# Projections as one float32 matmul per product, from a ring of 12 landed weight units

## The reference

```python
h = rms_norm(x, norm_mix)
proj = h @ w_in                      # 2048 x (512 + 256 + 64 + 3 * 1024)
# MLA heads: q and k, v from the two latents by w_q_b (512 x 1536) and w_kv_b (256 x 2048)
# stick-breaking heads: q, k, v straight from proj
x = x + concat(rms_norm(o_mla), rms_norm(o_sb)) @ w_out          # 2048 x 2048
x = x + softmax(q_mem k_mem) v_mem @ w_mem_o   # w_mem_q 2048x512, w_mem_kv 2048x1024, w_mem_o 512x2048
x = x + hierarchical_moe(rms_norm(x))          # 32 experts of 512, gate, up and down
y = rms_norm(x)
```

## Time and profile before

| | |
|---|---|
| time, median of 3 runs | 1455.09 us (1454.99 to 1457.09) |
| span of the profiled execution, first to last instruction | 1450.0 us |
| the profiled execution's own time | only its span is given |
| TensorE busy | 1082.5 us, 75% |
| VectorE busy | 540.3 us, 37% |
| ScalarE busy | 337.4 us, 23% |
| mean granted clock of TensorE | 0.893 of full |
| HBM read | 479.04 MB, 332 GB/s over the span |

### The profile page before, as it was taken

How to read it: one execution, slowest core, us unless ns; L and a number is a source line. 1 busy time by engine, 2 the same in 40 slices (tenths; PEclk the granted TensorE clock), 3 DMA queues, 4 the chain that set the end, 5 groups by cost and what they waited for, 6 DMA issues and landing times.

```text
span 1450.0 us, 21354 instructions
## 1 busy us (share of the span) xinstructions
PE 1082.5 (75%) x8717; PEld 643.9 (44%) x8717; DVE 540.3 (37%) x1120; ACT 337.4 (23%) x609; POOL 33.2 (2%) x90
## 2 busy tenths in 40 slices
PE   6999988998998968667656666667656665666665
PEld 5888867777887733222222222223222222222222
DVE  5444556565564433322222222222222222222323
ACT  5554455565444230100000000000000000000002
POOL 1000000110001000000000000000000000000000
PEclk9999999999999988988888888788888898788977
DMA  6766743222655789999999999999999999999996
GB/s 212 268 190 189 185 134 116 87 88 93 209 182 176 322 350 423 428 425 426 428 427 427 423 428 427 427 424 427 427 427 425 426 428 427 427 424 427 427 427 259
DMA packets 85379, 481.69 MB, mean 332 GB/s; under 512 B 10262, under 2 KB 20636, under 8 KB 51932
## 3 DMA queue, kind: packets, MB, share of 16 engines
q1 hardware_dynamic: 84272, 478.70, 82.5%
q10 hardware_dynamic: 876, 2.15, 0.4%
q0 software_dynamic: 192, 0.31, 0.2%
HBM read 479.04 MB, written 2.10 MB: 332 GB/s over the span
## 4 chain that ended last, share of the span: by engine, by line
DMA 47%; PE 41%; ACT 3%; DVE 3%; SPq 3%; issue 1%; POOL 0%; DVEq 0%; ACTq 0%; POOLq 0%
DMA gu<-in_w_up 29%; DMA down<-in_w_down 17%; PE ps L408 8%; PE ps L410 8%; PE ps L409 8%; PE ps L684 5%; PE ps L731 5%; SPq L323 2%; PE ps L665 2%; PE ps L388 1%; PE ps L674 1%; DVE w_lo L1066 1%; PE ps L483 1%; ACT x_slots L1015 1%; DMA x_res<-in_x 1%
## 5 line engine op out<-in xcount | busy, mean ns | idle before, releaser
L684 PE MATMUL ps<-gu,xe 128*32 128x256 f32 x4096 | 317.9, 479 | 232.8 <-DMA gu<-in_w_up 231.8
L684 PEld LDWEIGHTS ps<-gu,xe 128*32 128x32 f32 x4096 | 153.9, 137 | 417.7 <-DMA gu<-in_w_up 279.0
L1461 DVE TENSOR_TENSOR x_res<-ps,x_res 128x512 f32<-128x512 f32 x248 | 153.9, 683 | 406.9 <-PE ps L694 406.9
L408 PE MATMUL ps<-w_hi,a_hi 128*128 128x512 f32 (+1 forms) x552 | 220.5, 399 | 8.6 <-DVE w_lo L1066 3.6
L409 PE MATMUL ps<-w_lo,a_hi 128*128 128x512 f32 (+1 forms) x552 | 215.9, 391 | 0.0
L1066 DVE TENSOR_TENSOR w_lo<-w_raw,w_hi 128x1024 fp32r<-128x1024 f32 (+1 forms) x138 | 163.9, 1200 | 132.0 <-ACT w_hi L772 131.1
L410 PE MATMUL ps<-w_hi,a_lo 128*128 128x512 f32 (+1 forms) x520 | 202.7, 390 | 0.0
L772 ACT ACTIVATE w_hi<-w_raw 128x1024 fp32r<-128x1024 f32 (+1 forms) x138 | 141.8, 1038 | 150.6 <-PE ps L410 142.8
L1022 ACT ACTIVATE sg<-ps 128x128 f32<-128x128 f32 x32 | 8.9, 278 | 625.8 <-PE ps L684 625.8
L731 PE MATMUL ps<-down,turned 128*32 128x512 f32 x1024 | 122.8, 611 | 31.6 <-ACT turned L1028 24.4
L408 PEld LDWEIGHTS ps<-w_hi,a_hi 128*128 128x128 f32 x552 | 106.0, 192 | 29.8 <-ACT w_hi L772 2.5
(11 more groups left out here) (233 smaller groups left out, 685.7 us busy)
## 6 DMA issues: line engine op xcount, KB each, us to landing
gu<-in_w_gate SPq DMA_DIRECT2D x64, 2048.0 KB, 31.7
gu<-in_w_up SPq DMA_DIRECT2D x64, 2048.0 KB, 36.1
down<-in_w_down SPq DMA_DIRECT2D x64, 2048.0 KB, 24.6
w_raw<-in_w_in SPq DMA_DIRECT2D x56, 512.0 KB, 4.0
w_raw<-in_w_out SPq DMA_DIRECT2D x32, 512.0 KB, 4.2
w_raw<-in_w_mem_kv SPq DMA_DIRECT2D x16, 512.0 KB, 3.7
w_raw<-in_w_mem_q SPq DMA_DIRECT2D x8, 512.0 KB, 3.4
w_raw<-in_w_mem_o SPq DMA_DIRECT2D x8, 512.0 KB, 4.4
```

Source lines behind the costliest of these rows:

```text
L408: pe.matmul(acc[t][:, 0:n], xh, wh, start=(k == 0), stop=False)
L684: mm = pe.matmul(ps[5][j * SLOTS:(j + 1) * SLOTS, 0:2 * P].rearrange("s (m f) -> s m f", m=2), xe[:, k, :], gu[side][:, b, :, kk, j * P:(j ...
L1461: ins = ve.tensor_tensor(xs, ps[g][:, :], xs, ALU.add)
```

## The change

The products become one matmul of type float32, on weights as they landed and on activations in one copy. The rounding on ScalarE and the subtraction on VectorE go. The room of `w_raw`, `w_hi` and `w_lo` becomes one ring of 12 units, and SP refills a place when TensorE has used its unit. The turned activations are copied once: banks with an even number by ScalarE, with an odd one by VectorE. `a_hi` and `a_lo` become `a_even` and `a_odd`, two places for whole activations: mix, mem, memx and memo use the first, q, kv and out the second. The order of TensorE's work and all that lies behind the projections are the same.

```diff
-RING = 4
+RING = 12
...
-        a_hi = place("a_hi", [P, KD, SEQ], F32R)
+        a_even = place("a_even", [P, KD, SEQ])
         a_lo_at = at[0]
-        a_lo = place("a_lo", [P, KD, SEQ], F32R)
+        a_odd = place("a_odd", [P, KD, SEQ])
         w_at = at[0]
-        w_raw = place("w_raw", [P, RING, UK, UN])
-        w_hi = place("w_hi", [P, RING, UK, UN], F32R)
-        w_lo = place("w_lo", [P, RING, UK, UN], F32R)
+        w_ring = place("w_ring", [P, RING, UK, UN])
...
+        def copied(b):
+
+            return (S("odd_copied"), b // 2 + 1) if b % 2 else (S("even_copied"), b // 2 + 1)
...
                 if u >= RING:
-                    sp.wait_ge(S("w_split"), u - RING + 1)
-                dst = w_raw[:, u % RING, :, 0:chunk_cols(c)]
+                    sp.wait_ge(S("w_used"), u - RING + 1)
+                dst = w_ring[:, u % RING, :, 0:chunk_cols(c)]
...
                     if b >= 4:
-                        pe.wait_ge(S("split_lo"), 2 * (b - 4) + 2)
+                        pe.wait_ge(*copied(b - 4))
...
-                    pe.wait_ge(S("w_rounded"), u + 1)
-                    pe.wait_ge(S("w_split"), u + 1)
+                    pe.wait_ge(S(f"w_loaded{u % RING}"), landed(u))
                     for j in range(UK):
                         k = i * UK + j
                         for t in range(TT):
-                            xh = hi[:, a0 + k, t * P:(t + 1) * P]
-                            xl = lo[:, a0 + k, t * P:(t + 1) * P]
-                            wh, wl = w_hi[:, u % RING, j, 0:n], w_lo[:, u % RING, j, 0:n]
-                            pe.matmul(acc[t][:, 0:n], xh, wh, start=(k == 0), stop=False)
-                            pe.matmul(acc[t][:, 0:n], xh, wl, start=False, stop=False)
-                            mm = pe.matmul(acc[t][:, 0:n], xl, wh, start=False, stop=(k == kn - 1))
+                            mm = pe.matmul(acc[t][:, 0:n], a[:, a0 + k, t * P:(t + 1) * P],
+                                           w_ring[:, u % RING, j, 0:n], start=(k == 0),
+                                           stop=(k == kn - 1))
                     mm.then_inc(S("w_used"), 1)
...
-            def rounded(upto):
...
-                    sc.activation(w_hi[:, u % RING, :, 0:n], w_raw[:, u % RING, :, 0:n],
-                                  ACT.Copy).then_inc(S("w_rounded"), 1)
...
-            def split_head(name, g0, used=0, a0=0, hi=a_hi, k_from=0, k_to=None):
+            def copy_split(name, g0, used=0, a0=0, a=a_even, k_from=0, k_to=None):
...
+                for kk in range(k_from // 2, (kn if k_to is None else k_to) // 2):
+                    b = k0 // 2 + kk
+                    if b % 2 == 0:
+                        sc.wait_ge(S("split_turned"), b + 1)
+                        for i in range(2):
+                            k = 2 * kk + i
+                            ins = sc.activation(a[:, a0 + k, :], ps[4 + b % 4][:, i * SEQ:(i + 1) * SEQ],
+                                                ACT.Copy,
+                                                scale=1.0 if g0 is None else g_t[:, g0 + k:g0 + k + 1])
+                        ins.then_inc(S("even_copied"), 1)
...
-            def split_w(upto):
...
-                    ve.tensor_tensor(w_lo[:, u % RING, :, 0:n], w_raw[:, u % RING, :, 0:n],
-                                     w_hi[:, u % RING, :, 0:n], ALU.subtract).then_inc(
-                                         S("w_split"), 1)
```

More of the change, by code:

```diff
@@ L256, in chunk_out, with landed, last_bank @@
             return S("chunk_copied"), sum(1 for d in range(c + 1) if d not in BY_VECTOR)
+        def landed(u):
+            return sum(16 * (UK if len(unit_src(*UNITS[v])[0].shape) == 4 else 1)
+                       for v in range(u % RING, u + 1, RING))
+        def copied(b):
+            return (S("odd_copied"), b // 2 + 1) if b % 2 else (S("even_copied"), b // 2 + 1)
+        def last_bank(name):
+            return (SPLIT0[name] + SPLIT_K[name]) // 2 - 1
         def turned_dst(c):
@@ L390, in split_turn, with copied_upto, project_units @@
                     mm.then_inc(S("split_turned"), 1)
-            def project_units(c, units, a0=0, hi=a_hi, lo=a_lo):
+            def copied_upto(b):
+                pe.wait_ge(*copied(b))
+                if b >= 1:
+                    pe.wait_ge(*copied(b - 1))
+            def project_units(c, units, a0=0, a=a_even):
                 kn, n = chunk_tiles(c), chunk_cols(c)
@@ L793, in split_head @@
                     sc.wait_ge(S("w_used"), used)
-                for k in range(k_from, kn if k_to is None else k_to):
-                    b = (k0 + k) // 2
-                    sc.wait_ge(S("split_turned"), b + 1)
-                    i = k % 2
-                    sc.activation(hi[:, a0 + k, :], ps[4 + b % 4][:, i * SEQ:(i + 1) * SEQ], ACT.Copy,
-                                  scale=1.0 if g0 is None else g_t[:, g0 + k:g0 + k + 1]
-                                  ).then_inc(S("split_hi"), 1)
-            def heads_and_units(name, g0, unit, used=0, lag=3):
-                for kk in range(SPLIT_K[name] // 2):
-                    split_head(name, g0, 0 if kk else used, k_from=2 * kk, k_to=2 * kk + 2)
-                    rounded(unit + RING + kk - lag)
+                for kk in range(k_from // 2, (kn if k_to is None else k_to) // 2):
[8 more added lines that the diff above has]
+                        ins.then_inc(S("even_copied"), 1)
             def chunk_copy(c, dst, col=None):
@@ L851, in _ @@
             for c in range(Q_LAT, Q_PE):
-                rounded(UNIT0[c + 1] + RING)
                 if c == Q_LAT:
@@ L874, in _ @@
                     chunk_copy(c, lambda t: v_sb[:, t, n0:n0 + UN], SS_X)
-            split_head("q", 48, UNIT0[Q_PE])
-            split_head("kv", 52, UNIT0[Q_PE], a0=4)
+            copy_split("q", 48, a=a_odd)
+            copy_split("kv", 52, a0=4, a=a_odd)
             sc.wait_ge(S("rstd"), 3)
             for c in range(Q_PE, MEM_K):
-                first = c in (Q_PE, V_MLA + 1)
-                rounded(UNIT0[c + 1] + RING - first)
                 if c < V_MLA:
@@ L907, in _ @@
             steps = [0]
-            split_head("mem", 16, UNIT0[MEM_K], k_to=KD // 2)
+            copy_split("mem", 16, UNIT0[Q_PE], k_to=KD // 2)
             for i in range(HEADS + 1):
-                rounded(min(UNIT0[MEM_K] + 2 * i, UNIT0[W_OUT]) + RING)
                 if i == 4:
@@ L958, in _ @@
             memx_heads(3)
-            rounded(UNIT0[MEM_Q + 1] + RING)
             sc.wait_ge(S("rstd"), 6)
@@ L1059, in link, with copy_split @@
                 ve.wait_ge(S("vector_step"), steps[0])
[L1061 to L1087 removed]
+            def copy_split(name, g0, used=0, a0=0, a=a_even, k_from=0, k_to=None):
+                k0, kn = SPLIT0[name], SPLIT_K[name]
+                if used:
+                    ve.wait_ge(S("w_used"), used)
+                for kk in range(k_from // 2, (kn if k_to is None else k_to) // 2):
+                    b = k0 // 2 + kk
+                    if b % 2:
+                        ve.wait_ge(S("split_turned"), b + 1)
+                        for i in range(2):
+                            k = 2 * kk + i
+                            ins = ve.tensor_scalar(a[:, a0 + k, :], ps[4 + b % 4][:, i * SEQ:(i + 1) * SEQ],
+                                                   1.0 if g0 is None else g_t[:, g0 + k:g0 + k + 1], None,
+                                                   ALU.mult)
+                        ins.then_inc(S("odd_copied"), 1)
             def copy_turned(c):
@@ L1206, in _ @@
                     if h == 0:
-                        split_rest("mem", 16, k_to=KD // 2)
+                        copy_split("mem", 16, UNIT0[Q_PE], k_to=KD // 2)
                     ve.wait_ge(S("sb_log1p"), h + 1)
@@ L1233, in _ @@
                                        S("o_copied"), 1)
-            rests_and_units("out", 54, UNIT0[W_OUT])
+            copy_split("out", 54, UNIT0[MEM_K], a=a_odd)
             ve.wait_ge(S("head_squared"), 4 * HEADS)
@@ L1303, in _ @@
                                  ALU.mult).then_inc(S("mem_o_copied"), 1)
-            split_rest("memo", None, lo=memo_lo)
+            copy_split("memo", None, UNIT0[MEM_O])
             def router_copy(q):
```

105 lines of the change are left out of this document (30 added, 75 removed).

## The result

The changed kernel is slower: 1522.47 us (median of four runs, 1517.52 to 1524.9) against 1455.19 for the kernel before. The ratio is 1.0457 with a 95% interval of 1.0435 to 1.0479, +67 us. On the forecast's base (1455.09) that is 1521.6 us. The forecast was 1545.7 with a range from 1522 to 1568: right in its sign and in what makes it, but 23 to 24 us too high, and the result stands at the lower edge of the range, on the forecast's base 0.4 us outside it.

What follows compares the result with a forecast made beforehand. TensorE was taken to bound the projections and weight loads the expert loop, which moves as a block. Units +107.6, waits -15.0 and clock -2 us on 1455.09 gave 1545.7 us, range 1522 to 1568.

Steps and rivals of the forecast that it cites:

- What bounds it: TensorE bounds the projections, weight loads the expert loop; one microsecond in the projections is one microsecond of the whole.
- the term +107.6 us for the growth of the units: Projections: 130 units of 512 columns grow 0.80 us each, +104.0; 8 units of 320 columns grow 0.45 each, +3.6.
- The new price: Projections: one float32 matmul of 512 columns costs 0.880 us a product, 3.52 a unit; bounds 0.85 to 0.907 a product.
- The old price: Projections before: three matmuls at 0.2267 us each, 0.680 us a product of 512 columns, 2.72 us a unit.
- The waits: TensorE's waits for rounding, splits and copies, from the start to the memory output, shrink: -15.0 us, bounds -19 to 0.
- the chain over three engines in each head: Attention heads: chain over ScalarE, VectorE and GpSimd, idle 0.2 us at most, covered by longer units; priced at nothing.
- The clock: Matmuls run at the lower clock behind idle gaps; where two such gaps shrink, -2 us, bounds -4 to 0.
- The ring: At the start, the ring of 12 issues more loads at once behind the first on the same queue; priced at nothing.
- rivals 1 and 2: Weight loads in the open: new with float32, about 1640 us, chance 0.05; or already before, about 1451 us, chance 0.01.
- rival 3: The engines' waits are replaced by others, so the 15 us don't come: about 1563 us, chance 0.10.
- rival 4: Not slower: float32 at 512 columns takes fewer than four column times; at 3, 1423 us; chance 0.02.
- rival 5: The low end: product price 0.85 us and the clock back everywhere, +91 - 19 - 4, about 1523 us; chance 0.10.

Runs made afterwards that it cites:

- Experiment 6: Kernel before without the matmul of high activations by low weights, all splitting still done: 1366.44 us, ratio 0.9379.
- experiment 3: Changed kernel with each product as two float32 matmuls of half the columns: 1522.28 us, ratio 1.0471.
- Experiment 5: Kernel before with small float32 matmuls, results unused, in the places where TensorE waits: 1451.66 us, ratio 0.9980.
- experiment 8: Kernel before with rounding and splitting reordered, plus small float32 matmuls in the remaining waits: 1439.45 us, ratio 0.9890.
- experiment 2: Kernel before with one float32 matmul a product, all splits kept, ring freed by split: 1536.65 us; unaltered changed kernel on same chip: 1519.68 us.
- experiment 4: Changed kernel with a ring of 4 landed units instead of 12: 1527.94 us; again, 1525.28 us against 1519.68 on the same chip.

## Why the forecast was right in kind and too high in size

**What bounds it: right.** Nearly all of the loss lies before the last projection (68.5 of 71.0 us between the two spans), and the expert loop moved as a block; the 1.9 us that were added behind the last projection go with the lower clock at the first expert (0.72 against 1.00). Experiment 6 adds the limit of the rule.

**The step that failed is the term +107.6 us for the growth of the units.** It measured +83.8. Both prices in it were off: the new one too high, the old one too low on average. Another 3.3 us of the error are the base: I took the 5.1 us from the span to the median for what lies around a span, but that is 1.8, and the rest was the quick execution that was profiled.

**The new price: too high.** I took 0.880 us, between 0.871 and 0.889, "since L573 is the nearest row". It measured 0.858, near the lower bound that I had from the expert matmuls (0.85). The error is in "7.5 spacings, 0.445 us": the stream's first record carries 0.10 us that does not recur (experiment 3). The two ends of my bracket rested on the same faulty number. For 130 units that is 130 x (3.52 - 3.43) = 11.7 us too many.

**The old price: right in the dense chunks, too low on average.** 2.72 us held there, but taken over all 130 units of 512 columns, from the first start to the last plus one spacing, a unit of before lasted 2.83 us. That is 13.8 us which I did not take off, the larger of the two errors. The five slow stretches are 8.3 of it. Much of the rest comes where float32 work passes to float32r; the timeline of the kernel before behind a head's scores:

```profile
253.24 0.48 PE L408 MATMUL ps<-w_hi,a_hi 128*128 128x512 f32 x1
253.55 0.40 PE L409 MATMUL ps<-w_lo,a_hi 128*128 128x512 f32 x1
253.79 0.39 PE L410 MATMUL ps<-w_hi,a_lo 128*128 128x512 f32 x1
254.02 0.40 PE L408 MATMUL ps<-w_hi,a_hi 128*128 128x512 f32 x1
```

The spacings are 0.31, 0.24 and 0.23 instead of 0.227, so the unit takes 2.83 us until 256.07. Both units of this head show it (the second from 258.94 to 261.77). The changed kernel has one kind of matmul and lasts 3.45 us a unit over all 130. With KV_LAT's 8 units (2.15 for 1.76 us, +3.2) the units grew by 80.6 + 3.2 = 83.8 us, not 107.6. It is also why a head's period grew by 0.96 us and not by 1.6: its two units grew by 0.60 each.

**The waits: right.** Forecast -15.0, measured -14.9, place by place nearly as said: the start is 1.8 earlier (1.5 forecast), L495's wait went from 2.2 to 0.9, sb_a's from 2.2 to 1.3 with pt_mla's 0.8 gone, the turns of MEM_K and MEM_Q from 2.9 to 1.5 (1.9 forecast). What I priced at nothing, the chain over three engines in each head, gave a little as well: from L495 to L505 it took 0.63 us in seven heads and takes 0.33 from L502 to L512, its counterpart, 2.1 us in all.

83.8 - 14.9 = 68.9, against 68.5 measured. That fits more closely than the account is complete: those 2.1 us in the heads are not in it, but for 0.2, nor are some small additions such as 0.08 us for each head's scores.

**The clock: the size was off.** I took -2 us from two places. None of the five slow stretches was left in this profile. There is one new one behind the memory turns, whose unit lost 1.25 us (4.68 from 276.93 to 281.61 us), so about -7 of clock lies within the 83.8. Experiment 5 speaks for the idle of the waits as the cause of the old ones: with fillers in it they are gone, and in experiment 8 no slow spacing is left before the last projection. Where the one that is left falls differs by execution: in the second profile of the changed kernel (experiment 2) the unit behind the memory turns is fast, and the first unit of the kernel, which now follows its turns without the 1.48 us of idle, loses 1.1 us.

**The ring: priced at nothing, worth 5 to 6 us.** "The cover is that a unit lands about every 1.3 us and is used in 3.5" was true for the units. What I did not look at was what is queued behind them on SP. The deeper ring lets the first expert's weights out 26 us earlier (experiment 4).

**The rivals.** The weight loads stayed covered (rivals 1 and 2): twice the loads at half the columns cost nothing (experiment 3). The waits were not replaced (rival 3), and a float32 product has four column times (rival 4). The result came out near rival 5, the low end (about 1523), which had 0.10. Price and clock did go its way, but that the number fits is luck in part: its -19 for the waits did not come (14.9), and neither did its +91 for the units, which rests on the old price of 2.72.

## What to carry to other kernels

Where TensorE is the bound, compare what a stream of matmuls costs a product, not how much work the other engines lose: 325 us of ScalarE's and VectorE's work went and bought 17 us, while one float32 matmul at 0.858 us took the place of three float32r at 0.680. Some 13 of the 17 us lay in a handful of waits, and the old kernel became 15.4 us faster by moving some rounding calls and starting two chunks earlier. When reading a price off a merged row, take the first and the last record out; and take the old price as an average over the whole kernel and not from its best stretch, as slow stretches and switches between kinds of matmul belong to it. When a ring's release changes from "prepared" to "used", look at what is queued behind its last loads.

## What I had not expected of the hardware

- A float32 stream has 0.429 us a record of 512 columns and 0.2158 a record of 256, two records a matmul. At 0.417 ns a column that is two column times a column and about 2.5 ns beyond them; a float32r matmul has 0.2267 for 512, one column time a column and 13.4 ns beyond.
- Behind float32 work the first two spacings of float32r matmuls are 0.31 and 0.24 us instead of 0.227 (at 253.24 and 258.94 us).
- A change of an operand's height from 128 to 64 rows costs about 0.17 us each, and about as much in the changed kernel (2.74 us for the scores, 0.2 each by the same sum).
- A stretch at the lower clock level need not begin with the wait: in the kernel before, behind the 2.12 us of idle that ended at 444.81 us, the first five spacings were 0.23 to 0.31 us, and the slow ones began at 446.05. Behind the 1.69 us that ended at 195.52 the very first was slow.
